# Head norms in batches through compact rows, sample queries spread in one fp32r pass, and the convolution's gate product on GpSimd

## The reference, cut to what matters

```
h = RMSNorm(x);  z = h @ w_in
  z's columns: conv value a | conv gate b | dilated q,k,v (12 heads x 32)
             | MoBA q,k,v (4 heads x 64) | three gates of width 1024
u  = a * sigmoid(b)                       # gate product of the convolution
dq, dk, mq, mk = RMSNorm per head (x * rsqrt(mean over the head of x*x + 1e-6) * g)
A: causal depthwise convolution of u, 31 taps, LayerNorm, swish, projection
B: dilated attention, 3 groups of 4 heads; samples attend to stored keys
C: block-sparse attention, 4 heads; each sample scores all 2048 cached keys,
   takes the best 3 blocks of 256
x += (sum of sigmoid(gate) * branch) @ w_out
x += relu(RMSNorm(x) @ w_ff1)^2 @ w_ff2
```

## Time and profile before

| | us |
|---|---|
| median of 3 runs | 542.09 |
| lowest and highest run | 541.05, 545.58 |
| span of the profiled execution, first to last instruction | 541.1 |
| busy in it: PE, DVE, ACT, POOL | 484.2, 367.8, 233.2, 156.5 |
| bytes moved by DMA, mean rate | 130.87 MB, 242 GB/s |

### The profile page before, as it was taken

One profiled execution on the slowest core, in us unless ns is written; L12 is line 12 of the kernel. 1 busy time (PEld: TensorE's weight loads), 2 busy tenths in 40 slices (PEclk: granted clock), 3 DMA queues, 4 the chain that ended last, 5 costly groups with the idle time before them and its releaser, 6 DMA issues.

```text
span 541.1 us, 9293 instructions
## 1 busy us (share of the span) xinstructions
PE 484.2 (89%) x3669; PEld 443.0 (82%) x3669; DVE 367.8 (68%) x477; ACT 233.2 (43%) x428; POOL 156.5 (29%) x85
## 2 busy tenths in 40 slices
PE   3959996979859989978966998999999999999997
PEld 1848895869759769957654788899999999999997
DVE  3146999999999774799441685797777774444440
ACT  6344564225346424404175335744544443434330
POOL 4555563756547524702110506300000000000000
PEclk9969999789898969979996899999999999999999
DMA  9983775476936846716989926598898999699900
GB/s 284 381 289 117 270 275 177 180 271 230 354 111 213 260 156 222 250 74 253 342 337 351 311 89 223 161 306 303 246 354 294 282 305 282 234 254 306 294 11 20
DMA packets 86235, 130.87 MB, mean 242 GB/s; under 512 B 2806, under 2 KB 82076, under 8 KB 83620
## 3 DMA queue, kind: packets, MB, share of 16 engines
q1 hardware_dynamic: 82669, 93.99, 54.5%
q0 software_dynamic: 2992, 35.95, 17.7%
q10 hardware_dynamic: 543, 0.51, 0.3%
HBM read 128.05 MB, written 24.74 MB: 282 GB/s over the span
## 4 chain that ended last, share of the span: by engine, by line
PE 56%; DVE 21%; DMA 9%; issue 9%; ACT 3%; POOL 1%; SPq 1%; ACTq 0%; DVEq 0%
PE ps L943 34%; DVE ca L1362 6%; DVE kv L1326 5%; DMA raw<-in_w_in 5%; DMA kv<-in_cache_v,pidx 3%; PE ps L631 3%; PE ps L632 3%; PE ps L633 3%; DVE stdq L1317 3%; PE ps L760 2%; PE ps L821 2%; PE ps L852 2%; DVE sm L1330 1%; DMA raw<-in_w_out 1%; PE ps L692 1%
## 5 line engine op out<-in xcount | busy, mean ns | idle before, releaser
L575 POOL TENSOR_TENSOR rawlo<-raw,whi 128x1024 fp32r<-128x1024 f32 x53 | 131.4, 2493 | 113.5 <-ACT whi L1029 113.4
L631 PE MATMUL ps<-acts,whi 128*128 128x264 f32 x424 | 130.9, 309 | 18.3 <-POOL rawlo L575 12.6
L632 PE MATMUL ps<-acts,whi 128*128 128x264 f32 x424 | 125.7, 297 | 0.0
L633 PE MATMUL ps<-acts,rawlo 128*128 128x264 f32 x424 | 125.2, 295 | 0.0
L631 PEld LDWEIGHTS ps<-acts,whi 128*128 128x128 f32 x424 | 85.8, 202 | 26.1 <-POOL rawlo L575 14.7
L1622 DVE TENSOR_TENSOR ws<-fraw,ws 128x1024 fp32r<-128x1024 f32 x64 | 78.1, 1221 | 40.2 <-ACT ws L1224 40.1
L943 PE MATMUL ps<-as,ws 128*128 128x264 f32 x768 | 94.7, 284 | 0.0
L943 PEld LDWEIGHTS ps<-as,ws 128*128 128x128 f32 x768 | 93.3, 188 | 0.2
L943 PE MATMUL ps<-hs,ws 128*128 128x264 f32 x768 | 93.2, 284 | 0.0
L943 PEld LDWEIGHTS ps<-hs,ws 128*128 128x128 f32 x768 | 92.9, 188 | 0.1
L632 PEld LDWEIGHTS ps<-acts,whi 128*128 128x128 f32 x424 | 85.8, 202 | 0.1
(11 more groups left out here) (226 smaller groups left out, 523.2 us busy)
## 6 DMA issues: line engine op xcount, KB each, us to landing
fraw<-in_w_ff SPq DMA_DIRECT2D x32, 1024.0 KB, 8.1
raw<-in_w_in SPq DMA_DIRECT2D x14, 1536.0 KB, 8.2
out_dk_s<-in_state_dil_k SPq DMA_DIRECT2D x8, 1023.5 KB
out_dv_s<-in_state_dil_v SPq DMA_DIRECT2D x8, 1023.5 KB
raw<-in_w_out SPq DMA_DIRECT2D x2, 1536.0 KB, 8.8
ebias<-bias_rows SPq DMA_DIRECT2D x4, 512.0 KB, 7.6
out_dk_s<-in_state_dil_k SPq DMA_DIRECT2D x8, 255.5 KB
out_dv_s<-in_state_dil_v SPq DMA_DIRECT2D x8, 255.5 KB
```

Of the source, the lines that this page charges most:

```text
L575: pool.tensor_tensor(raw_unit(u, rawlo), raw_unit(u), whi[u % WR][:, :, :].bitcast(F32), ALU.subtract).then_inc(wlo_ready, 1)
L631: pe.matmul(out, hi, acts[0][:, k], start=k == 0, stop=False)
L632: pe.matmul(out, hi, acts[1][:, k], start=False, stop=False)
L633: return pe.matmul(out, lo, acts[0][:, k], start=False, stop=k == KD - 1)
```

## The change

Four things are changed.

- **Norms per head.** The ten groups are taken in four batches: (0, 1), (2, 3), (4, 5, 6), (7, 8, 9). The matmul over the squares now has 32 output columns instead of 128 and leaves one row per head (sums of `sum32` or `sum64`). The groups of a batch go to different 32-partition strips of one PSUM bank (`tile_position`). One ACT instruction and one DVE reciprocal handle the whole batch (64 or 96 partitions x 264, in `stdc`). A second, fp32 matmul per group (`expand`, with `spread32` or `spread64`) spreads the rows back to 128 partitions of PSUM. DVE multiplies the channels by it, now with that operand in PSUM. The places of both on PE are given by `MEAN_AT` and `EXPAND_AT`; DVE's list is written anew.
- **Sample queries.** ACT and DVE split the natural query rows once into an fp32r high part (partitions 0 to 7 of `q2`) and a low part (partitions 32 to 39). Each spread is then one fp32r matmul over 64 partitions with a column of `pickq`. The first two spreads move from unit 4 to unit 5.
- **Gate product.** It is made by POOL, in one piece for the samples and three pieces of 128x256, behind the low halves of units 23, 24 and 25. The taps on DVE wait for all of them.
- Buffers and constants to match.

```diff
@@ -56,8 +56,15 @@
+BATCHES = [(0, 1), (2, 3), (4, 5, 6), (7, 8, 9)]
+BATCH = [b for b, qs in enumerate(BATCHES) for _ in qs]
+MEAN_AT = {2: 0, 4: 1, 9: 2, 14: 3}
+EXPAND_AT = {3: (0, 1), 6: (2, 3), 12: (4, 5), 14: (6,), 17: (7, 8), 19: (9,)}
 OFF, _n = {}, 0
-for _k, _w in (("ident", P), ("eps", 1), ("sub8", 1), ("ones", P), ("bd32", P), ("bd64", P), ("blkT", P), ("blk", NB),
+for _k, _w in (("ident", P), ("eps", 1), ("sub8", 1), ("ones", P), ("sum32", DH), ("sum64", DH),
+               ("spread32", P), ("spread64", P), ("pickq", NS), ("blkT", P), ("blk", NB),
                ("hmask", HPG), ("mmask", 2 * MH), ("iota", NB), ("pick4", MH), ("pick16", 4 * HPG)):
@@ -94,8 +101,11 @@
     put("ones", np.ones((P, P)))
-    put("bd32", (p[:, None] // DH == p[None] // DH) / DH)
-    put("bd64", (p[:, None] // ME == p[None] // ME) / ME)
+    put("sum32", (p[:, None] // DH == np.arange(DH)[None]) / DH)
+    put("sum64", (p[:, None] // ME == np.arange(DH)[None]) / ME)
+    put("spread32", p[:, None] % DH == p[None] // DH)
+    put("spread64", p[:, None] % DH == p[None] // ME)
+    put("pickq", (p[:, None] < 2 * DH) & (p[:, None] % DH == np.arange(NS)[None]))
     put("blkT", np.arange(NB)[:, None] == p[None] // (P // NB))
@@ -189,7 +199,9 @@
         stv = sb("stv", [P, NG, NS, P], at=raw_at)
-        stdq = sb("stdq", [P, 4, T])
+        stdc = sb("stdc", [3 * DH, 2, T])
+        q2 = sb("q2", [2 * DH, 640], F32R)
+        pickq = sb("pickq", [2 * DH, NS], F32R)
         scv = sb("scv", [NS * HALO // 2, 2, C], at=probT_at)
@@ -338,9 +352,9 @@
-        NAT_AT = {3: (0, 1), 10: (2, 3), 11: (4,), 12: (5,), 15: (6, 7), 16: (8,), 20: (9,), 21: (10,), 22: (11, 12),
+        NAT_AT = {4: (0, 1), 10: (2, 3), 11: (4,), 12: (5,), 15: (6, 7), 16: (8,), 20: (9,), 21: (10,), 22: (11, 12),
                   23: (13, 14), 24: (15, 16), 25: (17, 18), 26: (19, 20)}
-        SPREAD_AT = {4: (0, 1), 8: (2,), 12: (3,), 16: (4,), 21: (5,), 27: (6,), 31: (7,), 33: (8, 9),
+        SPREAD_AT = {5: (0, 1), 8: (2,), 12: (3,), 16: (4,), 21: (5,), 27: (6,), 31: (7,), 33: (8, 9),
                      34: (10, 11, 12, 13, 14, 15)}
@@ -361,6 +375,14 @@
+        def square(q):
+            return rx[:, :] if q % 3 == 2 else squ[:, q % 3]
+        def expand_bank(q):
+            return (7, 6, 7)[q - BATCHES[BATCH[q]][0]]
@@ -575,11 +598,23 @@
+            def gate_sample():
+                pool.wait_ge(z_evac, U_G)
+                pool.tensor_tensor(usx[:, :, :, HALO], ca[:, :, SEQ:T], cb[:, :, SEQ:T], ALU.mult).then_inc(u_ready, 1)
+            def gate_prompt(c):
+                pool.tensor_tensor(uext[:, c, HALO:], ca[:, c, 0:SEQ], cb[:, c, 0:SEQ], ALU.mult).then_inc(u_ready, 1)
                 low(u)
+                if u == U_G + 2:
+                    gate_sample()
+                if 0 <= u - U_G - 2 < KC:
+                    gate_prompt(u - U_G - 2)
                 for s, at in enumerate(KV_AT):
@@ -642,13 +677,30 @@
-            def mean_square(q):
+            def mean_square(b):
                 pe.wait_ge(const_in, 16)
-                pe.wait_ge(sq_ready, q + 1)
-                if q >= 2:
-                    pe.wait_ge(std_done, q - 1)
-                bd = cst("bd64") if q < 4 else cst("bd32")
-                pe.matmul(ps[:, 6 + q % 2, 0:T], bd, squ[:, q % 2], start=True, stop=True).then_inc(ms_done, 1)
+                if b:
+                    pe.wait_ge(qn_done, BATCHES[b - 1][1] + 1)
+                for i, q in enumerate(BATCHES[b]):
+                    pe.wait_ge(sq_ready, q + 1)
+                    ins = pe.matmul(ps[i * DH:(i + 1) * DH, 6, 0:T], cst("sum64") if q < 4 else cst("sum32"), square(q),
+                                    start=True, stop=True, tile_position=(0, i * DH))
+                ins.then_inc(ms_done, 1)
+            def expand(q):
+                b = BATCH[q]
+                i = q - BATCHES[b][0]
+                pe.wait_ge(rstd_done, b + 1)
+                if i == 2:
+                    pe.wait_ge(qn_done, q - 1)
+                elif i == 0 and b:
+                    pe.wait_ge(qn_done, q)
+                rows = slice(i * DH, (i + 1) * DH)
+                name = "spread64" if q < 4 else "spread32"
+                pe.matmul(ps[:, expand_bank(q), 0:T], const[rows, OFF[name][0]:OFF[name][1]], stdc[rows, b % 2],
+                          start=True, stop=True).then_inc(expanded, 1)
@@ -672,14 +724,16 @@
                 else:
-                    pe.wait_ge(u_ready, 2)
+                    pe.wait_ge(u_ready, u + 2)
                     pe.transpose(ps[0:HALO, bank, 0:P], uext[:, u, SEQ:SEQ + HALO], ident)
-                pe.wait_ge(nat_evac, 2 if n < NS else N_Q)
+                pe.wait_ge(q2_ready, 1 if n < NS else 2)
+                if n == 5:
+                    pe.wait_ge(qn_done, len(QK))
@@ -688,8 +742,8 @@
                 lo, hi = (384, 640) if n < NS else (0, 384)
-                sel = ident[0:NS, n % NS:n % NS + 1].broadcast_to([NS, P])
-                pe.matmul(ps[:, SPREAD_BANK[n], 0:hi - lo], sel, qnat[:, lo:hi], start=True, stop=True).then_inc(qb_done, 1)
+                sel = pickq[:, n % NS:n % NS + 1].broadcast_to([2 * DH, P])
+                pe.matmul(ps[:, SPREAD_BANK[n], 0:hi - lo], sel, q2[:, lo:hi], start=True, stop=True).then_inc(qb_done, 1)
@@ -872,10 +926,10 @@
                 unit(j)
-                if 1 <= j <= 4:
-                    mean_square(j - 1)
-                if 7 <= j <= 12:
-                    mean_square(j - 3)
+                for q in EXPAND_AT.get(j, ()):
+                    expand(q)
+                if j in MEAN_AT:
+                    mean_square(MEAN_AT[j])
                 if j == 5:
@@ -1043,18 +1097,18 @@
                     q = QK.index(j)
-                    if q >= 2:
-                        sc.wait_ge(ms_done, q - 1)
+                    if q >= 3:
+                        sc.wait_ge(ms_done, BATCH[q - 3] + 1)
                 if j in Q_UNITS:
                     zr = reversed_tiles(z[:, 0:SEQ])
-                    sc.activation(squ[:, q % 2, 0:SEQ].rearrange("p (t c) -> p t c", c=P), zr, ACT.Square)
-                    sc.activation(squ[:, q % 2, SEQ:T], z[:, SEQ:T], ACT.Square).then_inc(sq_ready, 1)
+                    sc.activation(square(q)[:, 0:SEQ].rearrange("p (t c) -> p t c", c=P), zr, ACT.Square)
+                    sc.activation(square(q)[:, SEQ:T], z[:, SEQ:T], ACT.Square).then_inc(sq_ready, 1)
                     sc.copy(qkv[:, j, 0:SEQ].rearrange("p (t c) -> p t c", c=P), zr)
                 if j in QK:
-                    sc.activation(squ[:, q % 2], z, ACT.Square).then_inc(sq_ready, 1)
+                    sc.activation(square(q), z, ACT.Square).then_inc(sq_ready, 1)
                 if j < 15:
@@ -1064,11 +1118,22 @@
-            def deviation(q):
-                sc.wait_ge(ms_done, q + 1)
-                if q >= 4:
-                    sc.wait_ge(qn_done, q - 3)
-                sc.activation(stdq[:, q % 4], ps[:, 6 + q % 2, 0:T], ACT.Sqrt, bias=cst("eps")).then_inc(std_done, 1)
+            def deviation(b):
+                sc.wait_ge(ms_done, b + 1)
+                if b >= 2:
+                    sc.wait_ge(expanded, BATCHES[b - 2][-1] + 1)
+                r = len(BATCHES[b]) * DH
+                sc.activation(stdc[0:r, b % 2], ps[0:r, 6, 0:T], ACT.Sqrt, bias=cst("eps", r)).then_inc(std_done, 1)
+            def query_high(k):
+                lo, hi = ((384, 640), (0, 384))[k]
+                sc.wait_ge(nat_evac, (2, N_Q)[k])
+                if k == 0:
+                    sc.wait_ge(q2_clear, 1)
+                    sc.wait_ge(const_in, 16)
+                    sc.copy(pickq[:, :], cst("pickq", 2 * DH)).then_inc(q2_hi, 1)
+                sc.copy(q2[0:NS, lo:hi], qnat[:, lo:hi]).then_inc(q2_hi, 1)
@@ -1150,12 +1215,10 @@
                 take(j)
+                if j in MEAN_AT:
+                    deviation(MEAN_AT[j])
                 if j + WR < NU:
                     high(j + WR)
-                if 1 <= j <= 4:
-                    deviation(j - 1)
-                if 7 <= j <= 12:
-                    deviation(j - 3)
                 if j == 5:
@@ -1163,6 +1226,8 @@
                     natural_out(i)
+                if j in (4, 16):
+                    query_high(j // 16)
                 if j - 1 in SCORES_AT[:2]:
@@ -1309,13 +1374,25 @@
+            def invert(b):
+                v.wait_ge(std_done, b + 1)
+                r = stdc[0:len(BATCHES[b]) * DH, b % 2]
+                v.reciprocal(r, r).then_inc(rstd_done, 1)
                 g = par("mqn" if q < 2 else "mkn" if q < 4 else "dqn" if q < 7 else "dkn")
-                v.wait_ge(std_done, q + 1)
+                v.wait_ge(expanded, q + 1)
                 v.wait_ge(z_evac, u + 1)
-                step(v.reciprocal(stdq[:, q % 4], stdq[:, q % 4]))
-                v.scalar_tensor_tensor(qkv[:, u], qkv[:, u], g, stdq[:, q % 4], ALU.mult, ALU.mult).then_inc(qn_done, 1)
```

(41 more changed lines are left out.)

5 lines of the change are left out of this document (4 added, 1 removed).

## The result

| | before | changed |
|---|---|---|
| median of the runs on one chip, us | 543.52 (4 runs) | 546.12 (4 runs) |
| lowest and highest | 541.05, 545.58 | 544.86, 547.55 |
| span of the profiled execution | 541.1 | 544.2 |
| busy in it: PE, DVE, ACT, POOL | 484.2, 367.8, 233.2, 156.5 | 482.4, 342.5, 231.9, 159.6 |

The ratio of changed to before is 1.0151, with a 95% interval of [1.0084, 1.0218]: **slower by 1.5%**. All ratios here leave out the slow runs (over 1.5% above the fastest of the same kernel), and since the kernel before scatters widely, 532.8 to 548.4 us over all its runs, a ratio can differ from the quotient of two medians, which is 1.005 in this table. Both say slower, by 1.5% or by 0.5%. I had forecast 539 and "the same". DVE has 25 us less to do, as intended, and the kernel takes longer all the same.

The account below looks back on a forecast made before the run. It took DVE, never pausing up to the first tap, as the bound until 132 us, and PE's MLP matmuls from 349 us. 541.1 + 1.0 (first tap) - 2.8 (dilated scores) = 539.3, stated as 539; range 530 to 547.

Parts of the forecast that it names:

- Start: Product of sample 0 on DVE comes only after norms 2 and 3, at 54.4 us instead of 44.68: 9.7 us late.
- First loop: From sample 0's product through POOL's fetch and PE's unit 9 to DVE's second reciprocal, at 72.7 us; DVE idles 5 us.
- Second loop: Next fetch, low half and PE's unit 12, up to norm 4 at 86.5 us; DVE idles 7.5 us.
- Third loop: Low half and PE's units 16 and 17, up to norm 7 at 110.2 us; DVE idles 6 us.
- The query's low half with 0.5 of hold: DVE's small subtraction behind norm 9, at most 0.5 us of work, would be held by POOL for 0.5 us.
- First tap: DVE's first tap at 132.8 us instead of 131.78, 1.0 us lost, with 1 us of hold by POOL counted before it.
- Gate product neutral: Moving the gate product from DVE to POOL leaves the sum the same within 1 us.
- Dilated scores -2.8: At 189 to 197 us, one-pass query spreads let six DVE products take 3.3 us instead of 6.1, gaining 2.8.
- What it gains or loses there it keeps to the end: Any shift of the end of the first 200 us stays whole, since PE's MLP chain from 349 us is untouched.
- DVE stays the bound: Rival: waits on PE don't form up to the first tap, giving 522.5 us; chance 0.10.
- PE falls to its lower clock for longer: Rival: in units 9 to 21 slow units cost 2.2 us each, four further ones giving 548.1 us; chance 0.14.
- Still held: Rival: DVE's norm multiplications are held though an operand is in PSUM, giving 544 us; chance 0.04.

Follow-up runs that it names:

- e1: Changed kernel with product and sum of sample 0 put ahead of norms 2 and 3: 540.0 us, ratio 1.005 to the kernel before.
- e6: Changed kernel with the subtraction of the query's low half moved ahead of norm 7, from behind norm 9: 542.1 us, ratio 1.007 to the kernel before.
- e7: Kernel before with only the gate product moved to POOL: 540.0 us, ratio 0.993.
- e4: Kernel before with only the one-pass fp32r spreads of the sample queries: 538.1 us, ratio 1.001.
- e2: Changed kernel with only POOL's fetches moved later, to 10, 13, 18, 22, 25: 527.8 us, ratio 0.985 to the kernel before.
- e8: Changed kernel with fetches at 10, 13, 17, 21, 24 and the sum of sample 2 ahead of norm 6: 526.5 us, ratio 0.977 to the kernel before.
- e9: Kernel before, without batches, with reciprocal written to PSUM, one-pass query spreads and fetches at 10, 13, 18, 22, 25: 524.9 us, ratio 0.969.
- e3: Kernel before, norms one by one, with only the reciprocal written to PSUM: 529.0 us, ratio 0.983.
- e5: Kernel before with only POOL's fetches moved later, to 10, 13, 18, 22, 25: 529.6 us, ratio 0.982.
- e10: Kernel before with one-pass query spreads and gate product on POOL, no batches, fetches where they were: 539.3 us, ratio 0.992.

## Why the prediction was wrong

**The mechanism was right and two sizes were off, by 3.5 us each. They turned a forecast gain of 1.8 us in the span into a loss of 3.1.** By its own steps:

- *Multiplications no longer held*: right, 0.49 each.
- *Readings*: two slips change nothing in the walk. DVE's nine tenths begin with the fifth slice, 54 us, and the eight multiplications took 20.1 us together, not 17.6 (2.20 is the mean of all ten, with the two short ones at the start).
- *Start*: product 0 predicted at 54.4, measured 54.55. e1 shows that it counts: 3.9 us earlier there, 3.9 us earlier at the first tap.
- *First loop*: unit 9 taken as 4.4 us behind its pause; it ran wholly at 1.2 GHz and took 5.5. It began 0.5 later than predicted. Reciprocal at 74.44 instead of 72.7.
- *Second loop*: norm 4 at 88.00 (predicted 86.5). Unit 12, behind a pause of 2.9 us, took 3.1, less than the 3.6 I gave it. Norm 6 came 2.0 late.
- *Third loop*: unit 16 took 5.4 (predicted 4.9), and the transposes and the spread between it and unit 17 0.8, which I had left out. Norm 7 at 113.99 instead of 110.2, norm 9 at 120.65 instead of 117.1. **The loops together: +3.5 us.** That is the first term mis-sized; 1.6 of it are the two units at the lower clock, for which I had taken 4.4 and 4.9.
- *"The query's low half with 0.5 of hold"*: **this is the step that failed by most in a single term.** It was held for two low halves out of a run of three and took 4.46, in front of product 4: 3.5 more than the 1.0 in my sum. I had the row that shows this very thing, the 6.77 us behind three low halves of the earlier trace rows, and still let my bounds end at "a whole low half more", though I had the fetch release POOL just ahead of it. e6 puts 3.1 us on it at the first tap and 4.0 in the whole time.
- *First tap*: predicted 132.8, measured 138.93. The 1 us of hold that I had put in front of it did not occur; 3.5 + 3.5 less that 1 is the 6.1 us.
- *Gate product neutral*: right at the first tap (e7).
- *Dilated scores -2.8*: right in kind; the changed kernel is 7.9 us behind at the second logits (189.18 against 181.24) and 5.5 behind the products, a gain of 2.4. e4 has 3.1.
- *"What it gains or loses there it keeps to the end"*: wrong by 2.4 us in my favour. Of the 5.5 only 3.1 are left at the MLP. The windows of 290 to 300 us, before and then changed:

```profile
290.00:300.00 10.00, 8.16 (x45) 5.17 (x38) 1.12 (x5) 4.63 (x6) 2.33 (x2) 0.50 1.22 459
```

```profile
290.00:300.00 10.00, 6.29 (x72) 3.42 (x64) 1.44 (x4) 5.72 (x9) 0.00 (x0) 0.83 0.75 258
```

The kernel before ran this stretch at 1.2 GHz (0.50), the changed one mostly at the upper level. No run isolates this, so it is a reading and not shown.
- *"I say 539"*: a slip of scale. The sum, 539.3, is a span, and I set the span of 541.1 beside times of runs as if they were alike. A run's time is about 2 us longer than its span (546.16 against 544.2 in the changed kernel), so the sum should have been read as 541. The 7.1 us between 539 and 546.1 are 4.9 of span and 2 of this.

With these the sum reads 541.1 + 7.15 (first tap) + 0.5 (taps) - 2.4 (dilated) - 2.4 (later) = 543.9; the span is 544.2.

**The rivals.** "DVE stays the bound" did not happen, but its 522.5 was close to what e2 (527.8), e8 (526.5) and e9 (524.9) show once the loop is broken. "PE falls to its lower clock for longer" came out near the right time (548.1) by the wrong road, which is luck: two units at 1.2 GHz, not four further ones, and each time the next unit was back. PE paused three times, not four. The kernel that the Trainium skill describes there ("TensorE: Matmul & The Clock Gate", HAM oscillation) loses the clock at every wait; here it stayed at the upper level behind the pause of 2.9 us. "Still held" is out.

**What I did not see at all** is what e3 and e5 show. I took DVE's gapless work in the kernel before as its bound, found the hold, and asked only which operand causes it. But 10 us of it went when only the fetches moved (e5): POOL waits 9 us for a sum, low halves pile up, and the run that follows holds DVE, whose next sum is then late again. PE, which I had not counted among the bounds here, pauses for the late low halves, and its pauses are what goes in every faster kernel. The four corners:

| | fetches at 8, 11, 15, 20, 24 | at 10, 13, 18, 22, 25 |
|---|---|---|
| norms one by one | 541 to 543.5 (1) | 529.6 (0.982) |
| changed kernel | 546.1 (1.015) | 527.8 (0.985) |

By the ratios, in brackets, later fetches give 10 us in the one and 16 in the other (by the medians 11 and 18). e10 puts the changed kernel's extra loss at the early places on the batches. With the fetches right the two kernels can't be told apart: their runs overlap (528.1 to 532.4 and 526.7 to 531.3). What stays open is how the loss of the batches divides between PE's second matmul, the waits of the list and the late start: of the 9.9 us of the start e1 took back 3.9, and the 6 that stand beside the spread's move from unit 4 to unit 5 no run isolates.

## What to carry to other kernels

An engine that never pauses may still be waiting inside its instructions. Divide each group's busy time by the shortest duration of the same shape; if the quotient is far over one, ask who runs beside it, and why in such long runs, before taking work off the engine. An instruction that waits (here a fetch for a freed buffer) at the head of an in-order queue can cost twice, once for what stands behind it and once for the burst when it is let go; moving five fetches one to three places later was worth 10 us in the untouched kernel. A held instruction can be freed more cheaply than by batching: writing one operand to PSUM (e3) took 9 us off without touching the order. And when a small instruction is placed behind such a release, price its hold by the whole burst.

## What the runs showed of the hardware

- DVE's instructions with two SBUF operands did not merely wait for the current POOL instruction. They waited through back-to-back ones: 6.77 us behind a run of three, 6.82 in e10 within a run of four, 4.46 in the changed kernel within a run of three, where 0.5 is the free duration. The last two were let in one low half before the end of the run. In e5, where POOL pauses for 0.5 us between low halves, no multiplication took more than 2.71. The Trainium skill ("SBUF — State Buffer", Summary: rules for kernel authors) has the second to issue blocked "until the first finishes"; if the first is a single low half, a hold would end after 2.4 us, and the trace does not agree.
- The three sums of a batch, 32 output columns wide in different strips, ran in 0.65 us from the first start to the last end (72.61 to 73.26), where the fp32 sum of one group, 128 columns wide, takes 0.61: side by side, as predicted.
- A DVE reciprocal takes 1.79 us on 64, 96 or 128 partitions x 264 alike, and 1.81 on 128 when it writes to PSUM (e3).
- A unit behind a PE pause of 4.0 or 4.6 us ran at 1.2 GHz (granted clock 0.54 and 0.50, 5.5 and 5.4 us), one behind 2.9 us in 3.1 us at a granted clock of 1.00 (84 to 88 us).
